# Two-head scores over 64 rows each, DMA transposes in the loop, and the PSUM banks dealt anew, in a hybrid decoder layer on eight cores

## Chip, cores and metric

The kernel runs on all 8 cores of one Trainium2 chip (two dies of four cores). The metric is the device time in microseconds of the slowest core. The cores don't talk to each other: each computes half of one of the four sequences (4096 of 8192 tokens) and recomputes what it needs of the 2048 tokens before its half.

## What is computed

One decoder layer over x of 4 x 8192 tokens by 1024 channels:

```python
h = rmsnorm(x, g_mix)
q, k, v, u, qm = split(h @ w_in)            # 512, 512, 512, 256, 256 columns
# A) 8 heads of 64: causal dilated windows (128,1), (512,4), (2048,16), each a softmax
#    with ALiBi bias; the three merged by their softmax denominators
# B) trailing means over 2/4/8/16 tokens minus the token, times w_pool, times pool_scale
# C) 4 heads of 64: cross-attention into 256 memory tokens (rmsnorm(mem) @ w_mem_kv)
x = x + concat(A, B, C) @ w_out
a = relu(rmsnorm(x, g_ffn) @ w_ff1)         # 4096 wide
x = x + (a * a) @ w_ff2
return rmsnorm(x, g_final)
```

## The kernel before

A core walks over 12 tiles of 512 tokens: tiles 0 to 3 are the halo (only K and V are made), tiles 4 to 11 its own. There is no scheduler: the order in which the program is written is the order on every engine. A small tracker (`Tracker`, L50) puts semaphore waits before each instruction for what it reads and overwrites; TensorE never waits for itself. Every engine takes its instructions strictly in that order, and so does SyncE's queue (SP), which issues most DMAs.

**Tile j** has these parts in time:

- *Stage B* (L539): 16 groups of 8 matmuls (K = 128, 512 columns) for the projections, four groups for each of four 1 MB weight pieces. VectorE writes Q as bf16, scaled. Q is written twice: `QA` has heads of even number in rows 0 to 63 and zeros below, `QB` heads of odd number in rows 64 to 127 and zeros above (L564, L569; `qmA` and `qmB` at L582 and L587 for the memory heads). K lies with two heads over one another in 128 rows (`KT`). Hooks in stage B (L964 to L968, at groups 1, 4, 6, 8 and, for the last norm, 2) turn the normalised rows of the tile before (`hb`) into `h2T`, the FFN's input: `stage_J_pe`, L797.
- *The mix* (`slot_mix`, L911): 64 groups of 8 matmuls of the FFN of tile j-1, and between them the attention of tile j, item by item. A batch is four score matmuls of 128 columns (or one of 512 for the memory heads) into one PSUM bank, `exp` on ScalarE (L680), a multiplication by a mask on VectorE (L689), and four value matmuls into a bank `ob` (L706). A tile has 8 heads x 7 batches and 4 memory heads x 2. An item issues the front of batch i (scores, exp, mask) and the back (value matmuls) of batch i - lag. In the mix too, at g = 7, 21, 35, 49, the normalised rows of tile j+1 are transposed into `hT` (`stage_A_pe`, L507).
- *Stage IJ* (L806): the output projection, 8 groups of 8 matmuls.

**Transposes** are done by `transpose_to` (L425): for a chunk of 128 tokens 8 TensorE transposes of 128x128 into the one bank `tp`, then one VectorE copy. There are three `hb` buffers (L209); `hT` and `h2T` are one buffer each, with one record of readers and writers for all four chunks.

**PSUM** has eight banks: mm0, mm1, sc0 to sc2, ob0, ob1 and tp. The FFN takes mm0 and mm1 in turn, the scores the three sc banks (five, with mm, in tile 4, which has no FFN beside it), the value sums ob[h % 2]. In stages B and IJ all of mm and sc serve as targets.

**Weights** come in 1 MB bf16 pieces through a ring of three buffers. SP issues each load when TensorE has read the buffer's last piece (`ring_issue`, L377). Before that, during tiles 0 to 5, GpSimd's queue converts the fp32 weights to bf16 in DRAM by DMA. From tile 7 on x is loaded by GpSimd's queue (L287).

In the last tile no stage B stands between stage IJ and the FFN: the four chunks are transposed at L1004 to L1007, and then the FFN runs alone.

Of the kernel before, what the change touches and what calls it, by code (L numbers as in the profile page):

```python
# [122 lines left out]
def build_nc(n_own=NOWN, debug=False):  # L123
# [27 lines left out]
    with ExitStack() as es:  # L151
# [84 lines left out]
        scb = [psum(f"sc{i}", [128, 4, 128], F32) for i in range(3)]  # L236
        b_sc = [Buf(f"sc{i}") for i in range(3)]
# [3 lines left out]
        b_ob = [Buf(f"ob{i}") for i in range(2)]  # L241
# [297 lines left out]
        def stage_B(j, ghooks=None):  # L539
# [5 lines left out]
            for ip, pi in enumerate(plist):  # L545
# [5 lines left out]
                for ol in range(4):  # L551
# [11 lines left out]
                    if pi == 0:  # L563
                        T.op("dve", lambda: nc.vector.tensor_scalar(  # L564
                            out=QA[:, ol, :].rearrange("p (r c) -> p r c", r=4),
                            in0=m_[:, :].rearrange("p (c r) -> p r c", r=4), scalar1=csm_t[:, 5:6], scalar2=None,
                            op0=ALU.mult),
                            reads=[bm_, b_g], writes=[b_Q])
                        T.op("dve", lambda: nc.vector.tensor_scalar(  # L569
                            out=QB[:, ol, :].rearrange("p (r c) -> p r c", r=4),  # L570
                            in0=m_[:, :].rearrange("p (c r) -> p r c", r=4), scalar1=csm_t[:, 6:7], scalar2=None,
                            op0=ALU.mult),
                            reads=[bm_, b_g], writes=[b_Q])
# [6 lines left out]
                    else:  # L580
# [3 lines left out]
                            in0=m_[:, :].rearrange("p (c r) -> p r c", r=4), scalar1=csm_t[:, 5:6], scalar2=None,  # L584
                            op0=ALU.mult),
                            reads=[bm_, b_g], writes=[b_qm])
                        T.op("dve", lambda: nc.vector.tensor_scalar(  # L587
                            out=qmB[:, mp, :].rearrange("p (r c) -> p r c", r=4),
                            in0=m_[:, :].rearrange("p (c r) -> p r c", r=4), scalar1=csm_t[:, 6:7], scalar2=None,
                            op0=ALU.mult),  # L590
                            reads=[bm_, b_g], writes=[b_qm])
# [504 lines left out]
```

How the kernel before makes its waits and increments, by code:

```python
    def wait(self, e, tok):  # L61
        if tok is None:
            return
        sem, val, prod = tok
        if prod == "pe" and e == "pe":
            return
        key = (e, id(sem))
        if self.waited.get(key, 0) >= val:
            return
        self.waited[key] = val
        self.eng[e].wait_ge(sem, val)
        self.nwaits += 1
# [16 lines left out]
    def op(self, e, fn, reads=(), writes=(), mark=True):  # L89
        self._pre(e, reads, writes)
        ins = fn()
        self.ninst[e] += 1
        if mark:
            self.cnt[e] += 1
            ins.then_inc(self.sem[e], 1)
            tok = (self.sem[e], self.cnt[e], e)
        else:
            tok = (self.sem[e], self.cnt[e] + 1, e)
        self._post(tok, reads, writes)
        return tok
# [1 line left out]
    def dma(self, e, dsem, out, in_, reads=(), writes=(), **kw):  # L102
# [2 lines left out]
        self.ninst[e] += 1  # L105
        dsem.val += 16
        ins.then_inc(dsem.sem, 16)
        tok = (dsem.sem, dsem.val, "dma")
# [14 lines left out]
def build_nc(n_own=NOWN, debug=False):  # L123
# [878 lines left out]
                    mem_phase()  # L1002
        wide["on"] = False
        stage_J_pe(0)
        stage_J_end(NT - 1, 3)
        for tc in range(1, 4):
            stage_J_pe(tc)
        for f in ffn_items(NT - 1, None):
            f()
        for tc in range(NX1):
            nc.sync.wait_ge(out_sem[tc].sem, out_sem[tc].val)
        build_nc.stats = dict(ninst=dict(T.ninst), nwaits=T.nwaits, sbuf_left=nc.sbuf_bytes_remaining)
    return nc
```

## Time and profile before

| | us |
|---|---|
| median of 3 runs | 1693.33 (1692.15 to 1700.11) |
| the profiled execution, its own time | 1693.58 |
| its span, slowest core (1) | 1692.5 |
| spans of the eight cores | 1679.9 to 1692.5 |
| TensorE busy | 1587.7 (94%) |
| VectorE busy | 993.8 (59%) |
| ScalarE busy | 755.7 (45%) |
| a tile in the steady part (632 to 818) | 186.0 |

The span runs from the first to the last instruction of the slowest core; 1.1 us of the execution's time lie around it. A matmul's length in the trace includes its way through the array, so two that follow each other overlap: what one costs in a dense stream is the distance from start to start. "PEld" are the weight loads, which run beside matmuls. "L680" is line 680 of the kernel. The parts stand in the trace as: halo and the stage B of tile 4 to 140 us, its attention and output projection to 220, tile 5 to 445, tile 6 to 632, then one each 186 us, the last one's attention ending before 1561, and the lone FFN to the end.

### The profile page before, as it was taken

Reading aid. Unit: us, or ns where it says so; the run is one execution under the profiler, and the core shown is the slowest. Engines: PE = TensorE matmul, PEld = TensorE weight load, DVE = VectorE, ACT = ScalarE, POOL = GpSimd, SP = SyncE. Lnnn points to the kernel's source line nnn. Section 1 sums busy time; section 2 is a strip of 40 time slices with the busy share of each in tenths; the row PEclk is TensorE's granted clock in tenths of the full one; section 3 lists DMA queues with packets and bytes.
Section 4 is the critical chain, followed back from the end, with each engine's and each line's share of the span. In section 5 each row is a group of like instructions: output and inputs, shape, how many; then the busy total and the mean of one; then the engine's idle time right before and its main releaser. Section 6 shows DMA issues by size and latency. Waiting matters only on the chain.

```text
span 1692.5 us, 30487 instructions; the slowest of 8 cores (1679.9 to 1692.5 us)
## 1 busy us (share of the span) xinstructions
PE 1587.7 (94%) x10320; PEld 853.1 (50%) x10320; DVE 993.8 (59%) x1613; ACT 755.7 (45%) x1481; POOL 59.5 (4%) x103
## 2 busy tenths in 40 slices
PE   4897677899999999999999999999999999999997
PEld 2455433455455545554455545554555545554443
DVE  4557444555766566655676575665675575556344
ACT  3426613355345552546245543555255533555112
POOL 2000000000000000000000000000000010000000
PEclk9999788899999999999999999999999999999999
DMA  9999999963644455433635354435534373245343
GB/s 222 244 181 187 174 163 204 170 181 137 211 132 152 152 204 173 161 139 137 214 122 192 140 211 157 150 113 193 200 130 159 124 246 122 104 147 190 117 154 124
DMA packets 68950, 280.68 MB, mean 166 GB/s; under 512 B 6080, under 2 KB 27840, under 8 KB 46144
## 3 DMA queue, kind: packets, MB, share of 16 engines
q1 hardware_dynamic: 37008, 215.19, 37.6%
q0 software_dynamic: 31792, 63.54, 19.4%
q8 instruction: 87, 1.43, 0.3%
q14 instruction: 63, 0.52, 0.1%
HBM read 278.09 MB, written 39.85 MB: 188 GB/s over the span
## 4 chain that ended last, share of the span: by engine, by line
PE 84%; DMA 8%; DVE 3%; ACT 3%; issue 2%; SPq 0%; ACTq 0%; DVEq 0%; POOL 0%; POOLq 0%
PE mm L450 32%; PE mm L881 25%; PE sc L450 8%; PE ob L706 6%; PE sc L678 6%; DMA ring<-wscratch 6%; PE sc L814 4%; PE tp L427 2%; PE mm L814 1%; DMA ring<-w_in 1%; ACT tmp L403 1%; DVE hb L417 1%; ACT P L680 1%; DMA x<-xh 1%; DVE x L886 0%
## 5 line engine op out<-in xcount | busy, mean ns | idle before, releaser
L450 PE MATMUL mm<-h2T,ring 128*128 128x512 bf16 x2080 | 492.5, 382 | 12.3 <-DMA ring<-wscratch 11.3
L881 PE MATMUL mm<-ring,aT 128*128 128x512 bf16 x2048 | 475.8, 380 | 14.1 <-DMA ring<-wscratch 9.0
L680 ACT ACTIVATE P<-sc 128x512 bf16<-128x512 f32 x487 | 283.3, 595 | 240.2 <-PE sc L678 225.9
L862 DVE TENSOR_TENSOR aT<-tmp 128x512 bf16<-128x512 f32 x256 | 176.9, 691 | 249.5 <-ACT tmp L861 248.5
L450 PEld LDWEIGHTS mm<-h2T,ring 128*128 128x128 bf16 x2080 | 197.1, 99 | 220.9 <-issue 22.0
L881 PEld LDWEIGHTS mm<-ring,aT 128*128 128x128 bf16 x2048 | 192.9, 98 | 224.4 <-issue 27.0
L861 ACT ACTIVATE tmp<-mm 128x512 f32<-128x512 f32 x256 | 153.0, 598 | 326.2 <-PE mm L450 302.2
L886 DVE TENSOR_TENSOR x<-x,mm 128x512 f32<-128x512 f32 x256 | 175.6, 686 | 164.2 <-PE mm L881 159.1
L689 DVE TENSOR_TENSOR P<-P,E 128x512 bf16<-128x512 bf16 x448 | 186.0, 421 | 64.3 <-ACT P L680 62.3
L706 PE MATMUL ob<-P,Vd 128*128 128x128 bf16 x1792 | 177.0, 222 | 14.6 <-DVE P L689 14.4
L403 ACT ACTIVATE tmp<-x 128x1024 bf16<-128x1024 f32 x80 | 84.6, 1058 | 114.8 <-DVE x L819 54.3
L706 PEld LDWEIGHTS ob<-P,Vd 128*128 128x128 bf16 x1792 | 122.0, 100 | 21.9 <-issue 18.5
L450 PE MATMUL sc<-hT,ring 128*128 128x512 bf16 x488 | 112.6, 383 | 9.9 <-DMA ring<-wscratch 9.9
L678 PEld LDWEIGHTS sc<-QB,KT 128*128 128x128 bf16 x856 | 69.2, 110 | 40.6 <-issue 1.4
L537 ACT CAST Vd<-sc 128x512 bf16<-128x512 f32 x26 | 15.2, 586 | 164.2 <-PE sc L450 144.1
L814 PE MATMUL sc<-ring,yT 128*128 128x512 bf16 x384 | 87.8, 386 | 0.0
L678 PEld LDWEIGHTS sc<-QA,KT 128*128 128x128 bf16 x848 | 67.8, 110 | 39.6 <-issue 3.0
L450 PE MATMUL mm<-hT,ring 128*128 128x512 bf16 x344 | 83.5, 389 | 3.7 <-DVE hT L430 2.0
L678 PE MATMUL sc<-QB,KT 128*128 128x128 bf16 x856 | 83.9, 221 | 0.0
L678 PE MATMUL sc<-QA,KT 128*128 128x128 bf16 x848 | 81.7, 221 | 1.9 <-DVE QB L569 1.9
L427 PE MATMUL tp<-ident,hb 128*128 128x128 bf16 x656 | 53.6, 229 | 29.6 <-DVE hb L417 25.3
L450 PEld LDWEIGHTS sc<-hT,ring 128*128 128x128 bf16 x488 | 47.7, 99 | 66.2 <-issue 11.8
(99 smaller groups left out, 1224.3 us busy)
## 6 DMA issues: line engine op xcount, KB each, us to landing
ring<-wscratch SPq DMA_DIRECT2D x173, 1024.0 KB, 6.4
wscratch<-w_ff POOLq DMA_DIRECT2D x16, 1024.0 KB, 139.2
out<-x POOLq DMA_DIRECT2D x32, 512.0 KB, 5.8
x<-xh SPq DMA_DIRECT2D x28, 512.0 KB, 16.2
xa<-xh POOLq DMA_DIRECT2D x20, 512.0 KB, 6.5
x<-xh POOLq DMA_DIRECT2D x20, 512.0 KB, 8.6
Vd<-Vd SPq DMA_DIRECT2D x33, 192.0 KB, 5.9
xa<-xh SPq DMA_DIRECT2D x12, 512.0 KB, 15.5
```

The costliest lines, as they stand in the source:

```text
L403: T.op("act", lambda: nc.scalar.activation(out=jk[:].bitcast(BF16), in_=src, func=AF.Square, accum_out=ss), reads=[b_src], writes=[bs, bjk])
L427: T.op("pe", lambda: nc.tensor.transpose(tp[:, k * 128:(k + 1) * 128], hb[:, k * 128:(k + 1) * 128], ident[:]), reads=[b_hb, b_id], writes ...
L450: T.op("pe", lambda: nc.tensor.matmul(out_ap, lhsT=l, rhs=r, start=(i == 0), stop=(i == n - 1)), reads=reads, writes=[b_out], mark=(i == n ...
L678: T.op("pe", lambda: nc.tensor.matmul(o2, lhsT=l, rhs=r, start=True, stop=True), reads=bt["qk_reads"], writes=[bs_], mark=(i == n - 1))
L680: T.op("act", lambda: nc.scalar.activation(out=P_[:], in_=s_, func=AF.Exp, bias=bt.get("bias", 0.0)), reads=[bs_], writes=[bP_])
L689: T.op("dve", lambda: nc.vector.tensor_tensor(out=Pv, in0=Pv, in1=m, op=ALU.mult), reads=[bP_, b_E], writes=[bP_])
L706: T.op("pe", lambda: nc.tensor.matmul(oo, lhsT=l, rhs=r_, start=(bt["first"] and i == 0), stop=(bt["last"] and i == n - 1), skip_group_che ...
L814: T.op("pe", lambda: nc.tensor.matmul(m_[:], lhsT=yT[:, k, tc * 128:(tc + 1) * 128], rhs=pk[:, k, :], start=(k == 0), stop=(k == 7)), read ...
L861: T.op("act", lambda: nc.scalar.activation(out=rt[:], in_=m_[:], func=AF.Relu), reads=[bm_], writes=[brt])
L862: T.op("dve", lambda: nc.vector.tensor_tensor(out=aT[:, fl, :], in0=rt[:], in1=rt[:], op=ALU.mult), reads=[brt], writes=[b_aT[fl]])
L881: T.op("pe", lambda: nc.tensor.matmul(m_[:], lhsT=aT[:, fl, tc * 128:(tc + 1) * 128], rhs=rhs, start=(fl == 0), stop=(fl == 7)), reads=[b_ ...
L886: T.op("dve", lambda: nc.vector.tensor_tensor(out=xs, in0=xs, in1=m_[:], op=ALU.add), reads=[bm_], writes=[bx])
```

## The change

Three things change.

1. **Scores over 64 rows.** `QB` and `qmB` go; `QA` and `qmA` hold both heads, scaled by a constant. A score matmul of head h takes only its own 64 rows of K and Q (rows 0 to 63 for even h, 64 to 127 for odd). The batches of two heads form pairs; the front of a pair issues matmul i of the one and then matmul i of the other, into two banks. An item is now half a pair: one carries the front of pair i and the back of the first batch of pair i-1, the next one the back of the second batch. A tile has 32 pairs and 66 items (before 66 items of one batch each).
2. **PSUM.** Two sc banks and three ob banks (obank = h % 3); tile 4 has four score banks (two sc, two mm). The third bank ob2 takes the place of sc2 among the targets of stages B and IJ.
3. **DMA transposes.** For the chunks of tile 7 and later (`stage_A_pe`) and of the FFN input of tile 6 and later (`stage_J_pe`), SP issues one `dma_start_transpose` of a [128, 1024] chunk into `hT` or `h2T` instead. It waits for `hb` to be written and for what last wrote or read the target.

```diff
-        QB = sb("QB", [128, 4, TOK], BF16)
-        qmB = sb("qmB", [128, 2, TOK], BF16)
...
-        scb = [psum(f"sc{i}", [128, 4, 128], F32) for i in range(3)]
+        scb = [psum(f"sc{i}", [128, 4, 128], F32) for i in range(2)]
...
-        ob = [psum(f"ob{i}", [128, 4, 128], F32) for i in range(2)]
+        ob = [psum(f"ob{i}", [128, 4, 128], F32) for i in range(3)]
...
+        tr_sem = [dsem(f"trsem{i}") for i in range(NHB)]
+
+        def dma_transpose_to(hb, b_hb, dst3, b_dst):
+            i = [k for k in range(NHB) if b_hbs[k] is b_hb][0]
+            T._pre("sp", [b_hb], [b_dst])
+            ins = nc.sync.dma_start_transpose(out=dst3, in_=hb[:])
+            T.ninst["sp"] += 1
+            tr_sem[i].val += 16
+            ins.then_inc(tr_sem[i].sem, 16)
+            T._post((tr_sem[i].sem, tr_sem[i].val, "dma"), [b_hb], [b_dst])
...
-        mm_all += [(t_.rearrange("p a b -> p (a b)"), b_) for t_, b_ in zip(scb[:3], b_sc[:3])]
+        mm_all += [(t_.rearrange("p a b -> p (a b)"), b_) for t_, b_ in zip(scb[:2], b_sc[:2])]
+        mm_all += [(ob[2][:].rearrange("p a b -> p (a b)"), b_ob[2])]
...
         def stage_A_pe(j, c):
             h_, bh_ = a_hb.pop((j, c))
             hd, b_hd = hbuf(j)
-            transpose_to(h_, bh_, hd[:, :, c * 128:(c + 1) * 128], b_hd)
+            tr = dma_transpose_to if j >= NHALO + 3 else transpose_to
+            tr(h_, bh_, hd[:, :, c * 128:(c + 1) * 128], b_hd)
...
                         T.op("dve", lambda: nc.vector.tensor_scalar(
                             out=QA[:, ol, :].rearrange("p (r c) -> p r c", r=4),
-                            in0=m_[:, :].rearrange("p (c r) -> p r c", r=4), scalar1=csm_t[:, 5:6], scalar2=None,
+                            in0=m_[:, :].rearrange("p (c r) -> p r c", r=4), scalar1=0.125, scalar2=None,
                             op0=ALU.mult),
-                            reads=[bm_, b_g], writes=[b_Q])
-                        T.op("dve", lambda: nc.vector.tensor_scalar(
-                            out=QB[:, ol, :].rearrange("p (r c) -> p r c", r=4),
...
+                            reads=[bm_], writes=[b_Q])
...
-        def attn_items(j, lag, nsc):
+        def attn_items(j, nsc):
...
-                Qz = (QA if hh == 0 else QB)[:, pr, :]
+                p0 = 64 * hh
+                Qz = QA[p0:p0 + 64, pr, :]
                 v0 = pr * 192 + 64 * hh
-                o_ = ob[h % 2]
+                o_ = ob[h % 3]
...
-                        kv = KT[:, pr, slot * TOK:(slot + 1) * TOK].rearrange("p (a s) -> p a s", s=4)[:, :, r]
+                        kv = KT[p0:p0 + 64, pr, slot * TOK:(slot + 1) * TOK].rearrange("p (a s) -> p a s", s=4)[:, :, r]
...
+            def emit_front(bts):
+                fr = []
+                for bt in bts:
+                    si = cnt["sc"] % nsc
+                    cnt["sc"] += 1
+                    pi = cnt["P"] % NPB
+                    cnt["P"] += 1
+                    bt["P"] = (Pbuf[pi], b_P[pi])
+                    fr.append((bt, scb[si], b_sc[si]))
+                n = len(bts[0]["qk"])
+                for i in range(n):
+                    for bt, s_, bs_ in fr:
+                        sec, l, r = bt["qk"][i]
...
+                        T.op("pe", lambda: nc.tensor.matmul(o2, lhsT=l, rhs=r, start=True, stop=True),
+                             reads=bt["qk_reads"], writes=[bs_], mark=(i == n - 1))
+                for bt, s_, bs_ in fr:
+                    P_, bP_ = bt["P"]
+                    T.op("act", lambda: nc.scalar.activation(out=P_[:], in_=s_, func=AF.Exp, bias=bt.get("bias", 0.0)),
+                         reads=[bs_], writes=[bP_])
...
+            pairs = []
+            for a in range(6):
+                half = 7 if a < 4 else 2
+                base = 14 * a if a < 4 else 56 + 4 * (a - 4)
+                for i in range(half):
+                    pairs.append((batches[base + i], batches[base + half + i]))
             items = []
-            n = len(batches)
-            for i in range(n + lag):
-                def item(i=i):
+            n = len(pairs)
+            for i in range(n + 1):
+                def item0(i=i):
                     if i < n:
-                        emit_front(batches[i])
+                        emit_front(pairs[i])
                     flush_post()
-                    if i >= lag:
-                        emit_back(batches[i - lag])
-                items.append(item)
+                    if i >= 1:
+                        emit_back(pairs[i - 1][0])
+
+                def item1(i=i):
+                    flush_post()
+                    if i >= 1:
+                        emit_back(pairs[i - 1][1])
+                items += [item0, item1]
             return items
...
-        def stage_J_pe(tc):
+        def stage_J_pe(j, tc):
             h_, bh_ = j_hb.pop(tc)
-            transpose_to(h_, bh_, h2T[:, :, tc * 128:(tc + 1) * 128], b_h2T)
+            tr = dma_transpose_to if j >= NHALO + 2 else transpose_to
+            tr(h_, bh_, h2T[:, :, tc * 128:(tc + 1) * 128], b_h2T)
...
-            lag = 3 if first else 2
-            at = attn_items(j, lag, 5 if first else 3)
+            at = attn_items(j, 4 if first else 2)
```

## Rows read from the trace of the kernel before

**Rows 1.** The page: busy us of the engines, clock and DMA in slices.
```profile
PE 1587.7 (94%) x10320; PEld 853.1 (50%) x10320; DVE 993.8 (59%) x1613; ACT 755.7 (45%) x1481; POOL 59.5 (4%) x103
...
PEclk9999788899999999999999999999999999999999
DMA  9999999963644455433635354435534373245343
```

**Rows 2.** Busy us by stretch: PE, PEld, DVE, ACT, POOL; then clock, DMA share, GB/s.
```profile
265.00:350.00 85.00, 68.12 (x475) 38.27 (x476) 41.80 (x75) 33.66 (x63) 0.00 (x0) 0.88 1.00 187
632.00:818.00 186.00, 185.25 (x1235) 100.31 (x1236) 117.35 (x193) 89.78 (x174) 6.35 (x12) 1.00 0.47 163
```

**Rows 3.** PE's waits from 204 to 450 us: total, times, longest
```profile
PE mm L450 <- DMA ring<-wscratch: 11.3, 2, 7.6
PE sc L450 <- DMA ring<-wscratch: 9.1, 1, 9.1
PE mm L881 <- DMA ring<-wscratch: 9.0, 3, 5.3
```

**Rows 4.** PE's waits from 450 to 1540 us
```profile
PE mm L881 <- DVE x L886: 3.7, 6, 0.6
```

**Rows 5.** Timeline of PE inside a mix: start us, us, instructions
```profile
700.56 1.89 PE L450 MATMUL mm<-h2T,ring 128*128 128x512 bf16 x8
702.28 0.39 PE L678 MATMUL sc<-QA,KT 128*128 128x128 bf16 x4
702.51 0.39 PE L706 MATMUL ob<-P,Vd 128*128 128x128 bf16 x4
702.73 1.89 PE L450 MATMUL mm<-h2T,ring 128*128 128x512 bf16 x8
```

**Rows 6.** Timeline of the weight loads there
```profile
702.46 0.26 PEld L706 LDWEIGHTS ob<-P,Vd 128*128 128x128 bf16 x4
```

**Rows 7.** Groups by line and shape: busy us, mean ns of one, idle before
```profile
L678 PE MATMUL sc<-QB,KT 128*128 128x128 bf16 x856 | 83.9, 221 | 0.0
...
L678 PE MATMUL sc<-QA,KT 128*128 128x128 bf16 x848 | 81.7, 221 | 1.9 <-DVE QB L569 1.9
...
L427 PE MATMUL tp<-ident,hb 128*128 128x128 bf16 x656 | 53.6, 229 | 29.6 <-DVE hb L417 25.3 <-DVE h2T L430 4.4
...
L569 DVE TENSOR_SCALAR QB<-mm,csm_t 128x512 bf16<-128x512 f32 x16 | 12.0, 751 | 1.7
```

**Rows 8.** Timeline of PE at a memory-token score and value matmul
```profile
598.32 0.38 PE L678 MATMUL sc<-qmA,kmT 128*128 128x512 bf16 x1
...
598.54 0.38 PE L706 MATMUL ob<-P,vmA 128*128 128x512 bf16 x1
```

**Rows 9.** Timeline of PE around one transposed chunk in stage B
```profile
632.06 1.89 PE L450 MATMUL mm<-hT,ring 128*128 128x512 bf16 x8 [0.77 <-DMA ring<-wscratch]
633.79 0.61 PE L427 MATMUL tp<-ident,hb 128*128 128x128 bf16 x8
634.23 1.89 PE L450 MATMUL mm<-hT,ring 128*128 128x512 bf16 x8
```

**Rows 10.** Timeline of PE, first feed-forward group of that tile
```profile
661.47 1.89 PE L450 MATMUL mm<-h2T,ring 128*128 128x512 bf16 x8
```

**Rows 11.** DMA issues from 632 to 818 us: KB each, median us to landing
```profile
x<-xh POOLq DMA_DIRECT2D x4, 512.0 KB, 9.2
...
Vd<-Vd SPq DMA_DIRECT2D x4, 192.0 KB, 5.6
```

**Rows 12.** Copies between tiles in SBUF over the whole span
```profile
DMA to landing us min/median/max: 4.4/5.9/21.3
```

**Rows 13.** Timeline of PE after a long wait for a ring piece
```profile
237.04 3.57 PE L450 MATMUL sc<-hT,ring 128*128 128x512 bf16 x8 [9.13 <-DMA ring<-wscratch]
```

**Rows 14.** Timeline of PE at the last tile's transposes
```profile
1560.87 0.61 PE L427 MATMUL tp<-ident,hb 128*128 128x128 bf16 x8
...
1569.91 15.90 PE L450 MATMUL mm<-h2T,ring 128*128 128x512 bf16 x64 [1.01 <-DVE h2T L430]
```

More of the change, by code:

```diff
@@ L583, in stage_B @@
                             out=qmA[:, mp, :].rearrange("p (r c) -> p r c", r=4),
-                            in0=m_[:, :].rearrange("p (c r) -> p r c", r=4), scalar1=csm_t[:, 5:6], scalar2=None,
+                            in0=m_[:, :].rearrange("p (c r) -> p r c", r=4), scalar1=0.125, scalar2=None,
                             op0=ALU.mult),
[L586 to L591, printed above, removed]
+                            reads=[bm_], writes=[b_qm])
                 if own and (j > NHALO or ip == 0):
@@ L630, in attn_items @@
                                         meng="dve",
-                                        pv=pv, pv_reads=[b_Vd4[slot]], obank=h % 2,
+                                        pv=pv, pv_reads=[b_Vd4[slot]], obank=h % 3,
                                         first=(dl == 0), last=False, post=None))
@@ L656, in attn_items @@
                 mp, hh = mh // 2, mh % 2
-                Qz = (qmA if hh == 0 else qmB)[:, mp, :]
+                p0 = 64 * hh
+                Qz = qmA[p0:p0 + 64, mp, :]
                 v0 = mp * 192 + 64 * hh
                 for kc in range(2):
-                    batches.append(dict(qk=[(None, kmT[:, mp, kc * 128:(kc + 1) * 128], Qz)],
+                    batches.append(dict(qk=[(None, kmT[p0:p0 + 64, mp, kc * 128:(kc + 1) * 128], Qz)],
                                         qk_reads=[b_km, b_qm], mask=None, meng=None,
@@ L662, in attn_items @@
                                         pv=[(None, vmA[:, kc, v0:v0 + 128], None)],
-                                        pv_reads=[b_vm], obank=mh % 2, first=(kc == 0), last=(kc == 1),
+                                        pv_reads=[b_vm], obank=(8 + mh) % 3, first=(kc == 0), last=(kc == 1),
                                         post=(6 + mh // 2, hh) if kc == 1 else None))
-            def emit_front(bt):
-                si = cnt["sc"] % nsc
-                cnt["sc"] += 1
-                pi = cnt["P"] % NPB
-                cnt["P"] += 1
-                s_, bs_ = scb[si], b_sc[si]
-                P_, bP_ = Pbuf[pi], b_P[pi]
-                n = len(bt["qk"])
-                for i, (sec, l, r) in enumerate(bt["qk"]):
-                    o2 = s_[:, sec, :] if sec is not None else s_.rearrange("p a b -> p (a b)")
-                    if len(r.shape) == 3:
-                        o2 = o2.rearrange("p (a b) -> p a b", a=r.shape[1])
-                    T.op("pe", lambda: nc.tensor.matmul(o2, lhsT=l, rhs=r, start=True, stop=True),
-                         reads=bt["qk_reads"], writes=[bs_], mark=(i == n - 1))
-                T.op("act", lambda: nc.scalar.activation(out=P_[:], in_=s_, func=AF.Exp, bias=bt.get("bias", 0.0)),
-                     reads=[bs_], writes=[bP_])
-                if bt["mask"] is not None:
-                    m = bt["mask"]
-                    Pv = P_[:].rearrange("p (a b) q -> p a b q", a=2) if len(m.shape) == 4 else P_[:]
-                    if bt["meng"] == "pool":
-                        T.op("pool", lambda: nc.gpsimd.tensor_tensor(out=Pv, in0=Pv, in1=m, op=ALU.mult),
-                             reads=[bP_, b_E], writes=[bP_])
-                    else:
@@ new lines, in emit_front @@
+            def emit_front(bts):
[11 more added lines that the diff above has]
+                        sec, l, r = bt["qk"][i]
+                        o2 = s_[:, sec, :] if sec is not None else s_.rearrange("p a b -> p (a b)")
+                        if len(r.shape) == 3:
+                            o2 = o2.rearrange("p (a b) -> p a b", a=r.shape[1])
+                        T.op("pe", lambda: nc.tensor.matmul(o2, lhsT=l, rhs=r, start=True, stop=True),
[4 more added lines that the diff above has]
+                         reads=[bs_], writes=[bP_])
+                    if bt["mask"] is not None:
+                        m = bt["mask"]
+                        Pv = P_[:].rearrange("p (a b) q -> p a b q", a=2) if len(m.shape) == 4 else P_[:]
```

24 lines of the change are left out of this document (10 added, 14 removed).

## The prediction, made before the changed kernel ran

> **What bounds the kernel now.** I read the page first: TensorE is busy 94% of the span, VectorE 59%, ScalarE 45%. Its slices show two regimes: eight slices of 42.3 us in which the DMA engines are full and the granted clock falls below 1.0 at times, and then, to the end, a TensorE at nine tenths and DMA at three to six [rows 1]. The busy times by stretch say the same: up to 350 us DMA has a share of 1.00 and TensorE gaps, a steady tile (632 to 818) has TensorE busy 185.3 of 186 us, DMA at 0.47, VectorE at 117 [rows 2]. Who is waited for: between 204 and 450 us TensorE waits 29.4 us for ring pieces (11.3 + 9.1 + 9.0) [rows 3]; between 450 and 1540 us its longest wait is 3.7 us in all [rows 4]. So from about 350 us on only fewer TensorE slots shorten the kernel. Before that a saved slot mostly lengthens a wait for weights.
>
> What a slot is, the timeline shows, not the mean durations. In the mix 8 matmuls of 512 columns take 702.28 - 700.56 = 1.72 us, four of 128 columns 0.22 us (702.28 to 702.51 to 702.73) [rows 5]: 56 ns a matmul, though the group's mean says 221 ns [rows 7]. Their weight loads keep that pace, four in 0.26 us [rows 6]. A steady tile adds up from this: stages B and IJ and the FFN 88 groups x 1.73 = 152 us, 448 attention matmuls x 0.056 = 25.1, 16 memory matmuls x 0.22 [rows 8] = 3.5, 8 chunks of transposes x 0.45 = 3.6, together 184 of 186.
>
> **The change, part by part.**
>
> *Scores.* There are 856 + 848 score matmuls into sc, and 88 more into mm in tile 4, 1792 in all [rows 7], or 224 a tile: 224 x 0.056 = 12.5 us, and 8 memory scores x 0.22 = 1.7 us. Number and columns stay the same, only the rows halve. If the two halves of the array work side by side, half of the 14.2 us goes, 7.1 a tile; if they don't, nothing. I take 6.5 tiles (half of tile 5 lies past 350 us; 6 to 11 whole): 0 to -46 us. I choose the full overlap, since the loads already overlap each other [rows 6] and the alternating heads have other rows and other banks.
>
> *Entering and leaving the 64-row form.* Every front now sits between 128-row matmuls: 2 switches x 32 pairs x 6.5 tiles = 416. No row has one. Lower end: nothing. Upper end: the array runs empty at each, which is the part of a matmul that lies beyond its slot, 0.38 - 0.22 = 0.16 us [rows 8]: +67 us. I take one slot of 128 columns, 0.056 us, as the time for one wave to leave: +23 us. It is nearest in size to what changes, a short matmul. What the Trainium skill says here (TensorEngine Tiling (Array Packing), Key Properties) speaks against the change: switching the tiling mode, other than switching tiles, drains TensorE. By that rule, with the 0.16 us that a row gives for a way through the array, this term is +67 instead of +23; no row here shows a switch.
>
> *TensorE transposes.* A chunk costs 634.23 - 633.79 = 0.45 us of TensorE [rows 9]. Gone are stage A for tiles 7 to 11 (20 chunks) and stage J for tiles 6 to 10 (20): 40 x 0.45 = -18 us; four more in the last tile are counted below. The 44 copies out of tp and the 48 writes of QB and qmB (0.75 us each [rows 7]) leave VectorE. That is priced at nothing: TensorE hardly waits for VectorE in that part [rows 4], and without them it is only idler.
>
> *The DMA transposes in their place.* 256 KB from SBUF to SBUF each. Nearest row: the copies Vd<-Vd, also within SBUF and also SP's, 192 KB, 5.6 us in the steady tile; the longest median there is 9.2 us [rows 11], the extremes over the span are 4.4 and 21.3 [rows 12]. I take L = 5.6 us. In the mix they have 30 us and more until stage B reads hT: nothing. In stage B the four are a chain, since each waits for the last writer of h2T, that is, for its predecessor to land. SP's order is: first transpose (start of the stage), the ring load that waits for group 3, second, third, the ring load that waits for group 7, fourth, ring load for group 11, Vd copies, ring load. The second is issued at 7.2 us at the earliest (four groups of 1.73, and a little), and the fourth lands at 7.2 + 3L = 24.0 us. The FFN, which reads h2T, begins 661.47 - 632.06 = 29.4 us into the stage now [rows 9, 10], 27.6 without the four transposes. So at 5.6 us they are hidden with 3.6 us to spare, the limit being L = 6.8. Queued behind the third is the ring load for group 7, which may start at 14 us and is held to 7.2 + L = 12.8: no loss. VectorE's last norm waits for the first transpose to free its hb, 5.6 us into the stage, about when it runs now.
>
> *The last tile* has no such cover. Today it takes 1569.91 - 1560.87 = 9.0 us from the first transpose to the first FFN matmul [rows 14]. With the chain it is 4 x 5.6 = 22.4 us: +13.4 (L = 4.4: +8.6; L = 9.2: +27.8). The clock after such a pause is no new cost: 8 matmuls took 3.57 us after a 9.13 us wait [rows 13], the lower of the two levels, 1.2 GHz, but the last FFN starts slow today as well, 64 matmuls in 15.9 us instead of 13.8 [rows 14].
>
> *Pipeline and banks.* A front now asks for both sc banks. They were emptied by two exps of 0.6 us, and the next front comes two FFN groups later, 3.4 us: cover enough, and the value matmuls of a pair come as late. With three ob banks a head's bank is used again after its division has had three items. Tile 4 has no FFN beside it and goes from a lag of three batches to one pair; what it gains or loses stands in front of the 29.4 us of ring waits [rows 3]. All priced at nothing.
>
> **Sum:** 1693.6 (this execution; the median of the three runs is 1693.3, so no correction) - 46 - 18 + 23 + 13 = 1666 us.
>
> **Rivals.**
>
> *R1, the switches eat it (slower).* Place: both ends of each front. At 0.16 us each: 1693.6 - 46 - 18 + 67 + 13 = 1710. It decides from (46 + 18 - 13) / 416 = 0.12 us a switch; below that the kernel gains. For: loads today run ahead of the matmuls without a gap [rows 6], which only holds while the form stays the same. Against: the only thing that speaks for a full drain is outside this trace. 17%.
>
> *R2, no overlap (the change doesn't do what it says).* The 64-row matmuls follow each other at 56 ns as before, switching is free: 1693.6 - 18 + 13 = 1689. For: in the rows a matmul's slot is its columns and nothing else (0.22 for 4 x 128 as for 1 x 512) [rows 5, 8]. Against: nothing ties the second head's stream to the first's. 15%.
>
> *R3, long transposes.* If L is 9.2 us, the fourth lands at 7.2 + 27.6 = 34.8, 7.2 us late, in 5 tiles: +36; the end costs 27.8 instead of 13.4. With the score terms as forecast: 1693.6 - 46 + 23 - 18 + 36 + 28 = 1717. It decides from L = 6.8 us (late h2T) and is worse than before from about 8.0 us. For: the chain of four and the margin of 3.6 us. Against: the copy next to it takes 5.6 and moves three quarters as much. 10%. The Trainium skill gives two answers (VectorE: DVE Perf Modes, The three transpose paths: 1309 ns for a 128x128 block; Advanced Engine Details and Errata, X-Bar Transpose: as fast as regular DMAs). By the first, eight blocks one after another are an estimated 10.5 us, and the sum would be about 1740; by the second the forecast stands. No row here shows either.
>
> **How the numbers follow.** Forecast 58%, R1 17%, R2 15%, R3 10%. The forecast's own range is 1638 (free switches, L = 4.4) to 1689 (0.11 us a switch). The whole range reaches over R2 to R1 and the price of R3 above: 1638 to 1715; what is left out is a switch over 0.16 us and anything below free switches. 0.5% (8.5 us, about what a measurement can tell) parts the signs at 1685 and 1702: the forecast all but 3 points and a few of R2 are faster, 0.60; most of R2, and R1 with a switch of about 0.12, same, 0.15; R1 and R3 slower, 0.25.
>
> **What the profile after would show.** Right: in the mix the 8 score matmuls of a pair start within about 0.25 us, and the next 128-row matmul less than 0.1 us late on either side; a steady tile of 186 - 7.1 + 3.6 - 3.6 = 179 us; 1.73 us between groups of stage B; transposes landing in 4.4 to 6.8 us; some 22 us between the last IJ matmul and the lone FFN. Wrong: score starts 56 ns apart (R2); holes of 0.1 us or more before and after each front (R1); TensorE waiting for a DMA into h2T after stage B, or for ring pieces held back on SP (R3). New waits for exp or the ob banks would contradict what I priced at nothing.

## The result, and the profile after

| | before | after |
|---|---|---|
| median of 20 runs each, us | 1691.61 | 1700.24 |
| ratio | | 1.0051 (95%: 1.0028 to 1.0075) |
| profiled execution, us | 1693.58 | 1702.65 |
| its span, slowest core | 1692.5 (core 1) | 1701.6 (core 2) |

The ratios here and below leave out executions in a slower state, in which the cores of one die show a lower granted clock. The change costs 0.5%, where 1.6% less was forecast. The page after, busy time and slices (as in [rows 1]; the second line is TensorE's):

```profile
PE 1578.3 (93%) x9968; PEld 768.4 (45%) x9968; DVE 937.6 (55%) x1521; ACT 747.3 (44%) x1481; POOL 59.5 (3%) x103
...
PE   4897788899999999999999999999999989995897
...
PEclk9997689899999999999999999999999999998999
DMA  9999999963547456535846374646753583336333
```

TensorE is still the bound; behind 350 us it is clearly idle in two places, the slice from 1361 us (0.8) and the one from 1531 us (0.5). Where the 9.1 us of span come from, by the first matmul of each part in the two traces (the last column takes the median of the eight cores before and after, since the slowest core is not the same one):

| stretch | before | after | difference | of the medians |
|---|---|---|---|---|
| start to stage B of tile 4 (halo) | 105.7 | 108.8 | +3.1 | +0.2 |
| to stage B of tile 7 | 526.4 | 521.7 | -4.7 | +0.9 |
| to stage B of tile 11 (four tiles) | 743.6 | 734.5 | -9.1 | -9.0 |
| to stage IJ of tile 11 | 171.4 | 177.1 | +5.7 | +6.9 |
| to the lone FFN | 22.9 | 35.5 | +12.6 | +11.5 |
| to the end | 122.6 | 124.1 | +1.5 | +0.9 |

**The mix.** TensorE's timeline of the changed kernel at the place of [rows 5]:

```profile
700.35 1.89 PE L460 MATMUL mm<-h2T,ring 128*128 128x512 bf16 x8
702.17 0.41 PE L685 MATMUL sc<-QA,KT 64*128 64x128 bf16 x8
702.52 0.40 PE L710 MATMUL ob<-P,Vd 128*128 128x128 bf16 x4
702.75 1.89 PE L460 MATMUL mm<-h2T,ring 128*128 128x512 bf16 x8
```

The FFN's last slot ends at 700.35 + 1.73 = 702.07, the value matmuls begin at 702.52: 0.45 us for a pair's eight scores, what they took before (8 x 0.056). Inside it the time is spent otherwise. The last FFN matmul and the first score, by a narrow stretch of the same view:

```profile
701.86 0.38 PE L460 MATMUL mm<-h2T,ring 128*128 128x512 bf16 x1
702.17 0.24 PE L685 MATMUL sc<-QA,KT 64*128 64x128 bf16 x1
```

and the weight loads, a front's eight in 0.26 us, then none until the value matmuls, in the 128-row form again:

```profile
702.16 0.26 PEld L685 LDWEIGHTS sc<-QA,KT 64*128 64x128 bf16 x8 [0.42 <-issue]
702.51 0.23 PEld L710 LDWEIGHTS ob<-P,Vd 128*128 128x128 bf16 x4
```

The single records start at 702.170 and .173, .254 and .257, .310 and .313, .365 and .369, then 702.517: the two heads run side by side, 3 to 4 ns apart, and from the second two matmuls on, each two start 56 ns after the two before. That is the saving, 4 x 0.056 = 0.22 us. Against it stand 702.170 - 702.074 = 0.096 on entering, 0.084 - 0.056 = 0.028 behind the first two, 702.517 - 702.421 = 0.096 on leaving, 0.010 behind the first value matmul: 0.23 us for one round of entering and leaving. In [rows 6] the loads ran ahead of the matmuls; across a change of form none does (the 0.42 us before the first). The page TensorEngine Tiling (Array Packing) of the Trainium skill, Key Properties, says that changing the tiling mode drains TensorE. The trace agrees in that no load of the new form runs ahead and each change costs about 0.115 us. A full drain it doesn't show: the first score starts at 702.170, before the end of the last FFN matmul's record (701.86 + 0.38 = 702.24, though such ends are modelled).

**The DMA transposes.** The transposes into h2T (who waited for them, and landing times), and the waits of TensorE from 450 us on:

```profile
  DVE hb L415: 39.4, 6
  PE mm L460: 21.5, 1
...
DMA to landing us min/median/max: 3.0/4.9/14.7
```

```profile
PE mm L460 <- DMA h2T<-hb: 21.5, 1, 21.5
PE sc L460 <- DVE QA L575: 5.3, 1, 5.3
...
PE ob L460 <- DMA ring<-wscratch: 1.8, 1, 1.8
```

In the loop h2T was never late for the FFN. What is late is hb, the source: with three buffers the fourth norm of a tile needs the first one's buffer, and waits for its transpose to land. The timeline at the start of stage B of tile 11 (SPq is SP's queue; its lines span from the first issue to the end of the last):

```profile
1363.53 2.05 SPq L104 DMA_DIRECT2D ring<-wscratch  x2
...
1365.68 5.49 SPq L436 DMA_TRANSPOSE h2T<-hb  x1
...
1380.51 1.28 DVE L415 SCALAR_TENSOR_TENSOR hb<-x,stat,gb_ffn 128x1024 bf16<-128x1024 f32 x1 [11.02 <-DMA h2T<-hb]
...
1382.54 1.86 PE L460 MATMUL sc<-hT,ring 128*128 128x512 bf16 x4 [5.28 <-DVE QA L575]
```

Two ring loads (2 MB) are issued, the transpose stands right behind them and lands 14.7 us later; VectorE waits 11.0 us, the PSUM banks fill, TensorE waits 5.3 us and comes back at the lower clock level (four matmuls in 1.86 us, where eight take 1.89).

Two ring loads stand in front of the first transpose in every stage B, and yet it doesn't always land so late. What differs is what GpSimd's queue moves meanwhile:

| first transpose into h2T, in | issued at | landed after, us | on GpSimd's queue until then |
|---|---|---|---|
| stage B of tile 7 | 631.2 | 7.2 | nothing |
| stage B of tile 8 | 814.1 | 11.5 | three stores of `out` |
| stage B of tile 9 | 999.6 | 7.5 | nothing |
| stage B of tile 10 | 1182.7 | 8.0 | nothing |
| stage B of tile 11 | 1365.7 | 14.7 | two stores of `out`, three loads of x |
| last tile's end | 1556.6 | 11.3 | three stores of `out` |

Over the eight cores it landed in 7.2 to 9.6 us in the 19 cases with nothing there, and in 13.9 to 17.8 us in tile 11, with four to six such transfers. No run changed this traffic, so it is an association. Tile 8 has the stall in a smaller form: its stage B takes 29.9 us instead of 27.6, mainly because the ring load issued just before the first transpose takes 10.1 us to land, instead of 5.6 in tile 7, and TensorE waits 1.8 us for it (on the eight cores that stage takes 29.5 to 31.9 us). The end of the last tile:

```profile
1554.14 1.89 PE L830 MATMUL ob<-ring,yT 128*128 128x512 bf16 x8
...
1556.59 18.87 SPq L436 DMA_TRANSPOSE h2T<-hb  x4
...
1568.02 1.28 DVE L415 SCALAR_TENSOR_TENSOR hb<-x,stat,gb_ffn 128x1024 bf16<-128x1024 f32 x1 [9.05 <-DMA h2T<-hb]
1577.53 2.72 PE L460 MATMUL mm<-h2T,ring 128*128 128x512 bf16 x6 [21.49 <-DMA h2T<-hb]
```

The first, again behind ring loads, takes 11.4 us (1556.6 to 1568.0), the other three 9.5 together (to 1577.5).

### The profile page after: what moved, and what is told of

It is laid out like the page before. It is cut to its first block, busy times and chain, and to the rows that moved or that the text cites. A ratio compares the mean times of both kernels' runs of the same rounds, so it can differ in the third digit from the quotient of the medians.

```text
span 1701.6 us, 29917 instructions; the slowest of 8 cores (1690.3 to 1701.6 us)
## 1 busy us (share of the span) xinstructions
PE 1578.3 (93%) x9968; PEld 768.4 (45%) x9968; DVE 937.6 (55%) x1521; ACT 747.3 (44%) x1481; POOL 59.5 (3%) x103
## 2 busy tenths in 40 slices
DMA packets 115413, 292.19 MB, mean 172 GB/s; under 512 B 52544, under 2 KB 74304, under 8 KB 92608
## 4 chain that ended last, share of the span: by engine, by line
PE 80%; DMA 10%; DVE 3%; ACT 3%; issue 3%; SPq 0%; ACTq 0%; DVEq 0%; POOL 0%; POOLq 0%
PE mm L460 29%; PE mm L897 25%; PE ob L710 8%; DMA ring<-wscratch 5%; PE sc L460 5%; PE sc L685 4%; PE sc L830 3%; PE ob L460 3%; DMA x<-xh 2%; DMA h2T<-hb 2%; PE mm L830 2%; PE ob L830 1%; DMA ring<-w_in 1%; ACT tmp L877 1%; DVE aT L878 1%
## 5 line engine op out<-in xcount | busy, mean ns | idle before, releaser
L689 ACT ACTIVATE P<-sc 128x512 bf16<-128x512 f32 x480 | 260.1, 596 | 238.5 <-PE sc L685 232.0
L878 DVE TENSOR_TENSOR aT<-tmp 128x512 bf16<-128x512 f32 x256 | 177.1, 692 | 268.8 <-ACT tmp L877 267.5
L401 ACT ACTIVATE tmp<-x 128x1024 bf16<-128x1024 f32 x80 | 84.5, 1056 | 119.2 <-DVE x L835 54.4
L685 PE MATMUL sc<-QA,KT 64*128 64x128 bf16 x1680 | 88.6, 226 | 1.0 <-DVE QA L575 1.0
L685 PEld LDWEIGHTS sc<-QA,KT 64*128 64x128 bf16 x1680 | 53.8, 110 | 78.4 <-issue 75.8
L460 PE MATMUL sc<-hT,ring 128*128 128x512 bf16 x352 | 82.1, 385 | 5.4 <-DVE QA L575 5.3
L725 DVE TENSOR_TENSOR yT<-ob,tmp 64x512 bf16<-64x512 f32 x96 | 65.9, 686 | 12.9 <-ACT tmp L721 10.7
L548 ACT CAST Vd<-sc 128x512 bf16<-128x512 f32 x15 | 8.8, 585 | 145.8 <-PE sc L460 126.9
L719 ACT ACTIVATE tmp<-ob 64x512 f32<-64x512 f32 x96 | 56.7, 591 | 18.5 <-PE ob L710 16.6
L721 ACT ACTIVATE tmp<-tmp 64x512 f32<-64x512 f32 x96 | 60.3, 628 | 9.4 <-ACT tmp L719 0.7
L415 DVE SCALAR_TENSOR_TENSOR hb<-x,stat,gb_ffn 128x1024 bf16<-128x1024 f32 x32 | 40.9, 1279 | 39.4 <-DMA h2T<-hb 39.4
L830 PE MATMUL sc<-ring,yT 128*128 128x512 bf16 x256 | 59.4, 385 | 0.3 <-DVE yT L725 0.3
## 6 DMA issues: line engine op xcount, KB each, us to landing
x<-xh POOLq DMA_DIRECT2D x20, 512.0 KB, 12.1
```

The source lines that it names most:

```text
L401: T.op("act", lambda: nc.scalar.activation(out=jk[:].bitcast(BF16), in_=src, func=AF.Square, accum_out=ss), reads=[b_src], writes=[bs, bjk])
L460: T.op("pe", lambda: nc.tensor.matmul(out_ap, lhsT=l, rhs=r, start=(i == 0), stop=(i == n - 1)), reads=reads, writes=[b_out], mark=(i == n ...
L685: T.op("pe", lambda: nc.tensor.matmul(o2, lhsT=l, rhs=r, start=True, stop=True), reads=bt["qk_reads"], writes=[bs_], mark=(i == n - 1))
L689: T.op("act", lambda: nc.scalar.activation(out=P_[:], in_=s_, func=AF.Exp, bias=bt.get("bias", 0.0)), reads=[bs_], writes=[bP_])
L725: "dve", lambda: nc.vector.tensor_tensor(out=yT[lo:lo + 64, ychunk, :], in0=of[lo:lo + 64, :], in1=rc[lo:lo + 64, :], op=ALU.mult),
L830: T.op("pe", lambda: nc.tensor.matmul(m_[:], lhsT=yT[:, k, tc * 128:(tc + 1) * 128], rhs=pk[:, k, :], start=(k == 0), stop=(k == 7)), read ...
```

## Experiments

All ratios are to the kernel before, with 95% intervals. "Early" means that the transposes into h2T are issued as soon as their rows are ready, "no chain" that they don't wait for each other. There are three hb buffers where nothing else is said. "The mix" below is the stretch from the first matmul of a stage B to the first of stage IJ, 172.1 us before (transposes included), 169.2 after.

| kernel | ratio |
|---|---|
| changed | 1.0051 (1.0028 to 1.0075) |
| a1, TensorE transposes | 1.0020 (1.0011 to 1.0029) |
| a2, old scores, DMA transposes | 1.0030 (1.0018 to 1.0042) |
| a3, last tile by TensorE | 0.9998 (0.9989 to 1.0008) |
| a4, four hb | 1.0029 (1.0005 to 1.0052) |
| b1, heads not alternating | 1.0077 (1.0064 to 1.0090) |
| b2, fronts (the score matmuls of a pair) split in two | 1.0347 (1.0333 to 1.0360) |
| b3, 128 rows | 1.0107 (1.0087 to 1.0127) |
| b4, early issue | 1.0126 (1.0113 to 1.0139) |
| d1, no chain, four hb | 0.9977 (0.9967 to 0.9987) |
| d2, old scores, no chain, early | 0.9940 (0.9926 to 0.9954) |
| d3, pairs, no chain, early, four hb | 0.9996 (0.9987 to 1.0006) |
| d4, two pairs a front, no chain, early, four hb | 1.0056 (1.0043 to 1.0069) |
| e1, pairs, no chain, early in the last tile alone, four hb | 0.9923 (0.9898 to 0.9949) |
| e2, old scores, the same, three hb | 0.9949 (0.9934 to 0.9964) |

### The two halves of the change (a1, a2)

```diff
-            tr = dma_transpose_to if j >= NHALO + 3 else transpose_to
+            tr = transpose_to
```

(and the same in `stage_J_pe`).

> The changed kernel with all transposes back on TensorE; scores, pairs and banks as changed. Theory 1 (the scores are a draw: two heads overlap and save 4 x 0.056 = 0.22 us a pair, entering and leaving the 64-row form costs 0.096 + 0.028 + 0.096 + 0.010 = 0.23 us): a ratio to the kernel before of 0.999 to 1.004, a steady tile of 186 to 187 us, no wait for h2T. Theory 2 (the new order of items, the shorter lag or the banks cost time of their own): 1.006 or more, with new waits of TensorE for exp, masks or value banks.

1.0020, a steady tile of 186.0 to 186.4 us against 185.9. The scores are a draw, slightly on the losing side: 32 x (0.454 - 0.448) = 0.2 us a tile. In the profiles more than that stands in tiles 4 and 5 (+1.6 and +1.5 us, medians of the eight cores); why is not shown. a2 puts only `dma_transpose_to` into the kernel before:

> The kernel before with only the DMA transposes. Theory 1 (they save 2.9 us in each of five steady tiles, lose 12.6 us in the last tile, and now and then stall VectorE when the first one lands late behind two ring loads): 15 less, 13 to 20 more, so a ratio to the kernel before of 0.998 to 1.005. Theory 2 (the scores cost time of their own): below 0.998. In either, a steady tile of about 182 us.

1.0030, with a steady tile of 182.3 us: the transposes take 3.6 us from it, as forecast, and the changed kernel's 183.0 is 0.7 above that. TensorE waits 9.1 us for QB and 20.3 at the end. The parts add up, within intervals of this size: 0.0020 + 0.0030 = 0.0050, measured 0.0051. Both lose a little.

### The end and the stall (a3, a4)

```diff
-            tr = dma_transpose_to if j >= NHALO + 2 else transpose_to
+            tr = dma_transpose_to if NHALO + 2 <= j < NT - 1 else transpose_to
```

(in `stage_J_pe`)

> The changed kernel with the last tile's four chunks transposed by TensorE, the others by DMA as changed. If the serial chain at the end is where the gain goes, about 12 us come back: a ratio to the kernel before of 0.996 to 0.999. Rival (the end would be as long anyway, by the norms that come one after another): 1.003 to 1.006, like the changed kernel.

0.9998: 0.0053 x 1692 = 9.0 us of the 12 come back. (In its profile the stall of tile 11 was 6.2 us.)

```diff
-NHB = 3
+NHB = 4
```

> The changed kernel with four hb buffers instead of three, so that VectorE's last norm of a tile doesn't wait for the first DMA transpose to land. If these stalls (39.4 us of VectorE, one of which held TensorE for 5.3 us in the changed kernel's profile) cost time, 2 to 7 us come back: a ratio to the kernel before of 0.999 to 1.004. In the last tile it changes nothing, since the four transposes still follow each other. Rival (the stalls are covered): as the changed kernel, 1.003 to 1.007.

1.0029, some 4 us less, though the intervals overlap. The trace is clear: no wait of VectorE for a transpose to land, and the mix of tile 11 takes 169.2 us instead of 177.1. The late ring piece in tile 8 stays (3.2 us), and so does the end:

```profile
PE mm L460 <- DMA h2T<-hb: 20.7, 1, 20.7
```

### What the 64-row form costs and gives (b1, b2, b3, d4)

b1 issues one head's four matmuls and then the other's:

```diff
-                for i in range(n):
-                    for bt, s_, bs_ in fr:
+                for bt, s_, bs_ in fr:
+                    for i in range(n):
```

> The changed kernel with the four score matmuls of the first head issued one after the other and then those of the second; same 64-row forms, same banks, same number of switches. If the alternation is what makes the halves overlap, the overlap is nearly all lost: 0.224 us a pair for 28 pairs and 0.216 for 4 memory pairs (which are single matmuls and alternate as before, so perhaps not lost), over 6.5 to 7 tiles about +40 us: 1.02 to 1.03. Rival (the halves overlap whatever the order, or don't overlap): 1.003 to 1.007, as the changed kernel.

The rival holds. TensorE's timeline of b1 is that of the changed kernel:

```profile
701.31 0.42 PE L685 MATMUL sc<-QA,KT 64*128 64x128 bf16 x8
701.66 0.40 PE L710 MATMUL ob<-P,Vd 128*128 128x128 bf16 x4
```

Eight in 0.35 us again, and the single starts still come in twos, 13 ns apart, so matmuls of the two row halves overlap even when four of one are issued before four of the other. (Of the eight, the two that raise a semaphore, the fourth and the last issued, are the last two to start.) The alternation is worth 10 ns a front: the mix is 169.4 to 169.5 us in an undisturbed tile, against 169.1 to 169.4. That is 0.001 of the 0.0026 by which b1 is slower; the intervals of the two overlap.

b2 puts the four value matmuls of an item (`mid`, the back of the first batch of pair i-1) between the halves of a front:

```diff
                 for i in range(n):
+                    if i == 2 and mid is not None:
+                        mid()
+                        mid = None
                     for bt, s_, bs_ in fr:
```

> The changed kernel with each front of the 28 attention pairs cut in two, with the four value matmuls of 128 rows between the halves, so that the 64-row form is entered and left twice instead of once. If a round of entering and leaving costs 0.23 us, 28 x 0.23 = 6.4 us are added to a steady tile, over 6.5 tiles 42 us: a ratio to the kernel before of 1.025 to 1.035. Rival (the 0.1 us holes beside a front belong to its semaphore waits, not to the change of form): less than 1.012.

1.0347: the mix 174.9 us, 5.7 more in a tile for 28 more rounds, 0.20 us each. Timeline of b2:

```profile
702.23 1.89 PE L905 MATMUL mm<-ring,aT 128*128 128x512 bf16 x8
704.05 0.28 PE L688 MATMUL sc<-QA,KT 64*128 64x128 bf16 x4
704.27 0.40 PE L715 MATMUL ob<-P,Vd 128*128 128x128 bf16 x4
704.60 0.28 PE L688 MATMUL sc<-QA,KT 64*128 64x128 bf16 x4
704.82 1.90 PE L905 MATMUL mm<-ring,aT 128*128 128x512 bf16 x8
```

Four scores, which side by side are worth 2 x 0.056 us, take 0.22 us, and from the first value matmul to the next score it is 0.33 us instead of 0.22. Tile 4, without FFN, grows too, by 15 us, which is the rest.

b3 has 128 rows again (`QB`, `qmB` and their writes restored, K unsliced):

```diff
-                Qz = QA[p0:p0 + 64, pr, :]
+                Qz = (QA if hh == 0 else QB)[:, pr, :]
```

> The changed kernel with scores over 128 rows again (QA and QB with zeros, written twice), everything else as changed: pairs, alternation, banks, DMA transposes. If the 64-row form is a draw, the time stays as with it: a ratio to the kernel before of 1.001 to 1.006, the 8 score matmuls of a front 56 ns apart and no hole of 0.1 us beside them. Rival (the new order costs time and the 64-row form gains it back): above 1.008. Other rival (the 64-row form costs on balance): below 0.999.

1.0107, which meets the number of the first rival. Its mix is 169.1 us in an undisturbed tile, as after; the scores of a front, alone and in sequence (three of nine lines):

```profile
702.37 0.22 PE L697 MATMUL sc<-QA,KT 128*128 128x128 bf16 x1
702.42 0.22 PE L697 MATMUL sc<-QB,KT 128*128 128x128 bf16 x1
...
702.81 0.61 PE L722 MATMUL ob<-P,Vd 128*128 128x128 bf16 x8
```

702.37 to 702.81, 0.45 us, without holes. Order, banks and semaphore waits are those of the changed kernel, so its holes belong to the change of form. What b3 loses against the changed kernel is in stage B, in TensorE's waits:

```profile
PE mm L462 <- DMA h2T<-hb: 22.3, 1, 22.3
PE sc L462 <- DVE QB L582: 14.7, 4, 7.7
```

With two Q writes a group VectorE comes out of the stall behind the late transpose later, four times instead of once. Against b3, then, the 64-row form gains through the 48 writes that VectorE no longer makes, which I had priced at nothing. That this takes the DMA transposes, which stall VectorE, is argued: 128 rows in pairs with TensorE's transposes were not run. Against a2 the changed kernel gains nothing. a2 has the same 48 writes, transposes and three hb as b3 and differs from it in the order of the items and the banks; it is 0.0077 below b3 and 0.0021 below the changed kernel. So the rival's reason, that the new order costs time, stands: 0.6 us of it shows in the undisturbed mix (168.5 us in a2), the rest in stalls that are longer in b3, by what is not shown.

d4 enters the form half as often: 16 scores a front, four sc banks (tp in one of them), two value banks, eight P buffers (they hold the exps), on the transposes of d3 below:

```diff
+            quads = [pairs[2 * i] + pairs[2 * i + 1] for i in range(len(pairs) // 2)]
...
+                        if b == 0 and i < n:
+                            emit_front(quads[i])
```

> The same transposes, and fronts of two pairs: 16 score matmuls over 64 rows into four sc banks (tp shares the fourth, ob has two), eight P buffers, so that the 64-row form is entered and left 16 times a tile instead of 32. If a round of entering and leaving costs 0.23 us whatever stands between, 16 x 0.23 = 3.7 us go from a steady tile: against one pair a front 22 to 26 us less, a ratio to the kernel before of 0.974 to 0.982, and in the mix 16 score matmuls in about 0.68 us. Rival (bursts of four exps and masks, or two value banks, make TensorE wait): the gain is half or less, with waits for masks or value banks in the mix.

1.0056, where 0.974 to 0.982 was expected. Timeline of d4, and TensorE's longest wait in it from 450 to 1540 us:

```profile
668.08 1.89 PE L465 MATMUL mm<-h2T,ring 128*128 128x512 bf16 x8
669.90 0.64 PE L690 MATMUL sc<-QA,KT 64*128 64x128 bf16 x16
670.47 0.82 PE L465 MATMUL mm<-h2T,ring 128*128 128x512 bf16 x3
```

```profile
PE ob L715 <- DVE yT L730: 24.2, 25, 1.7
```

The front takes 670.47 - 668.08 - 1.73 = 0.66 us for 16, where two fronts of a pair take 0.91: the price of the form is per entry, as said. But the mix stays at 170 to 171 us: with two value banks TensorE waits 24.2 us for divisions in six tiles, 4.0 a tile, more than the 16 x 0.23 = 3.7 that was to be gained. Tile 4 lost 9 us against d3. With three value banks there is no room for four sc banks beside mm; that version was not tried.

### Where the transposes stand (b4, d1, d2, d3, e1, e2)

b4 issues them when their rows are ready:

```diff
                             stage_J_end(j, tc - 1)
+                            if j >= NHALO + 2 and tc < 3:
+                                stage_J_pe(j, tc - 1)
-            ring_issue()
-            ring_issue()
+            if j < NT - 1:
+                ring_issue()
+                ring_issue()
+            if j >= NHALO + 2:
+                stage_J_pe(j, 2)
```

> The changed kernel with the FFN-input transposes issued as soon as their rows are normalised: the first two inside stage IJ, ahead of its two ring loads, the third right after those, the fourth at group 4 of stage B; in the last tile all four ahead of the ring loads. If the first transpose is late because it lands behind 2 MB of ring loads, and the end is the serial chain, then the stall of VectorE goes (3 us or so) and the end shrinks from 21.5 us of waiting to about 8: a ratio to the kernel before of 0.992 to 0.997. Rival (a transpose takes its 5 us and more wherever it stands): 1.000 or more.

1.0126, where 0.992 to 0.997 was expected. The stall is gone and the end shorter, but TensorE waits for the ring in every stage B (its waits, then SP's timeline at one):

```profile
PE ob L460 <- DMA ring<-wscratch: 19.7, 5, 7.4
PE mm L460 <- DMA h2T<-hb: 12.3, 1, 12.3
```

```profile
813.32 10.59 SPq L436 DMA_TRANSPOSE h2T<-hb  x2
824.06 0.94 SPq L104 DMA_DIRECT2D ring<-wscratch  x2
```

SP holds the second transpose until the first has landed, and the two ring loads, issued at 811.99 in the changed kernel, go at 824. I had looked at the place in the DMA queue and not at SP behind it. So d1 takes the chain away (the four write different columns; readers wait for all four), with four hb:

```diff
-            T._pre("sp", [b_hb], [b_dst])
+            T._pre("sp", [b_hb], [])
+            for t in b_dst.r:
+                T.wait("sp", t)
+            ws = [] if b_dst.r else b_dst.ws + [b_dst.w]
...
+            b_dst.ws = ws
```

> The changed kernel with four hb buffers, and a DMA transpose that no longer waits for its predecessor into the same h2T or hT (the four write different columns; readers wait for all four). Places of issue as changed. If the chain of landings is what fills the last tile, its four transposes follow each other at the 1.25 us that SP needs for one instead of 3.75 us, behind the ring loads: the wait before the lone FFN falls from 21 to 8 to 14 us, and the kernel by 7 to 13 us against the one with four hb buffers alone (1.0029): 0.995 to 0.999. Rival (the transposes are slow because the ring loads are ahead of them, and waiting together doesn't help): 1.002 to 1.004.

0.9977, 8.8 us less than a4; the wait at the end is 15.1 us instead of 20.7 (8 to 14 was expected). No stage B stalls by more than 1.6 us on any core, and the mix of tile 11 is 169.2. This is the first gain over the kernel before. d2 and d3 have the early issue of b4 without the chain, d2 on the kernel before with three hb, d3 on the changed one with four:

> Scores, banks and lag of the kernel before; DMA transposes without the chain, issued as soon as the rows are normalised (first two inside stage IJ ahead of the ring loads, third behind them, fourth at group 4 of stage B; in the last tile all ahead of the ring loads). If SP's waits for landings were what held back the ring loads when the transposes stood early (ring waits of 1.7 to 7.4 us in each stage B), these are gone: 5 tiles x 3 us less, last tile as before or 2 us less: a ratio to the kernel before of 0.988 to 0.993. Rival (the transposes take bandwidth from the ring whatever SP does): 0.998 or more.

> The same transposes with the changed kernel's scores (two heads over 64 rows, one pair a front) and four hb buffers. If the 64-row scores are a draw, this is as fast as with the old scores, up to 0.003 slower as it was with TensorE transposes: 0.988 to 0.996. Rival (they gain once VectorE is relieved in stage B): faster than with the old scores by over 0.003.

0.9940 and 0.9996, each just above what was expected. The wait at the end falls to 7.5 us in both. But ring waits remain (d2, then d3):

```profile
PE sc L467 <- DMA ring<-wscratch: 9.7, 3, 7.9
```

```profile
PE ob L466 <- DMA ring<-wscratch: 9.0, 2, 6.1
```

That left open whether the early issue in the loop costs them. e1 is d3 with it in the last tile alone (`if j == NT - 1 and tc < 3`), e2 the same with the old scores and three hb:

> The changed kernel with four hb buffers and no chain, and the transposes moved ahead of the ring loads in the last tile alone; in the loop they are issued at the hooks of stage B, as changed. If moving them ahead inside stage IJ costs the loop ring waits (9.0 us in the profile with the pairs, and 1.8 for the clock), while in the last tile it gains 7.5 us of waiting (15.1 to 7.5), this beats both kernels it is made of (0.9977 and 0.9996): 0.991 to 0.995, with less than 2 us of ring waits after 450 us. Rival (the ring waits come with the DMA transposes wherever they are issued): 0.996 or more.

> The same places of issue and no chain with the scores of the kernel before, and three hb buffers, for which alone there is room beside QB. VectorE's last norm then waits again for the first transpose, which lands behind two ring loads, with two Q writes a group behind it. If that stall is what the score form decides (9.1 us of TensorE waiting for QB with the DMA transposes alone, none with four buffers), this is slower than with the pairs and four buffers, by 2 to 10 us: 0.993 to 0.999. Rival (the pairs cost 0.002 to 0.005 here as well): faster than the other by 0.002 or more.

e1 0.9923, e2 0.9949; the intervals overlap. TensorE's waits in e1, then e2:

```profile
PE mm L466 <- DMA h2T<-hb: 7.5, 1, 7.5
...
PE ob L466 <- DMA ring<-wscratch: 1.3, 1, 1.3
```

```profile
PE sc L467 <- DVE QB L587: 11.9, 3, 7.9
```

e1 is below both kernels, by 0.8% and 1.3%. With the pairs the early issue in the loop costs time (d3 against e1), and belongs where nothing queues behind it. With the old scores it costs none (d2 0.9940, e2 0.9949): there it pays for its ring waits by ending the wait for QB, 11.9 us in e2 and none in d2. Whether e1 leads e2 by its scores or by its fourth hb is open, since the old scores with four hb and no chain were not run.

d3 is 0.006 above d2, when a1 gives the pairs only 0.002. Of the 7.2 us between the medians of the eight cores 4.8 lie in tile 8: its stage B takes 29.4 to 32.4 us in d3, with a ring piece late on every core, and 27.6 to 28.6 in d2. Why only there and only with the pairs is not settled.

## Why the prediction was wrong

- **The regime** was read right. From 204 to 450 us the ring waits are of the same kind and size (10.8 + 7.6 + 7.9 = 26.3 us against 29.4 [rows 3]), and from there on TensorE's slots set the time, but for the stalls below.
- **The overlap of the two heads**, -46 us: right, the starts are 3 to 4 ns apart. Of my reasons, the alternation hardly counts (b1).
- **The switches**: this step failed. "I take one slot of 128 columns, 0.056 us" measured 0.115 us (0.23 a round in the trace, 0.20 by b2). 416 x 0.115 = +48 us instead of +23. R1 was priced with 0.16 and was to decide from 0.12; the truth lies just under that point, so the scores come out at -46 + 48, nothing. No row had the term, and "the time for one wave to leave" was too little: no weight load runs ahead across a change, and the first matmul of the new form comes 0.096 us late, with 0.01 to 0.03 more behind it. The 0.16 us [rows 8] of a full drain would have been nearly as far off on the other side. R1 had the place and the sign right.
- **TensorE's transposes**: right, a steady tile lost 3.6 us by them alone (a2) and 2.9 in the changed kernel. "The copies are priced at nothing", and the writes of QB too: wrong once VectorE stalls (b3: TensorE waits 14.7 us for it against 5.3).
- **Their landing**: L = 5.6 us as one number was the second failed step. The range is 3.0 to 14.7 into h2T (5.9 to 14.5 into hT), by what else is moving. The fourth came in time, since the later ones of the chain are short. But "VectorE's last norm waits for the first transpose ..., about when it runs now" took the 5.6 for the one transpose that stands behind two ring loads, and that one took 7.2 at the least. Tile 11 took 5.7 us more to its stage IJ, where 1.8 less was to come from the transposes and 3.5 less from the scores.
- **The last tile**: +13.4 forecast, +12.6 measured, which is luck: not four equal landings of 5.6, but 11.4 and then 9.5 for three.
- **Pipeline and banks** at nothing: right in the loop as far as waits show (no new one for exp, masks or value banks above 1 us in all from 450 us on), but b3 against a2 leaves a cost of the new order that no term had. Tile 4 takes 1.6 us more (113.8 us against 112.2, medians of the eight cores), at a granted clock of 0.66 against 0.83 from 150 to 200 us.

With the measured switch the sum is 1693.6 - 46 - 18 + 48 + 13 = 1691, against 1702.7 measured. Of the 12 us between, about 10 are the stalls of tile 11 (+5.7 instead of -1.8) and of tile 8 (2.4). The rest is small: the 0.7 us by which each steady tile falls short, the start, 3.1 us more on another core, and what tiles 4 to 6 give back. The time lies in the whole range, where R1 is, on the wrong side of no change: R1's cost at a smaller price, plus a part of R3's cause, long landings, in another place.

## What to carry to other kernels

Halving the rows of small matmuls to run two at once pays only if the run in that form is long: here 8 matmuls of 128 columns save 0.22 us and pay 0.23 us to enter and leave, 16 save 0.45 and pay about the same once (d4's front; the kernel around it lost that again). A DMA that replaces engine work brings its landing into whatever reuses its source, and that landing depends on what its own queue issued just before and, it seems, on what other queues move; count buffers for it, and don't chain transfers that write different columns. Before moving a transfer forward, see what stands behind it on the issuing queue.

## What was unexpected of the hardware

- Two streams of matmuls on the two row halves overlap although one head's four are issued wholly after the other's (b1: starts 13 ns apart, eight in 0.35 us).
- A DMA transpose of [128, 1024] bf16 landed in 3.0 us at best, and behind two 1 MB loads in 7.2 to 14.7. It takes 1.2 us of SP at best, up to 5.5 behind them (7.6 in a4). The page VectorE: DVE Perf Modes of the Trainium skill (The three transpose paths) gives 1309 ns for a 128x128 block; eight one after another would be an estimated 10.5 us, which the 3.0 us contradict.
- The DMA packets of the core rose from 68950 to 115413, 1056 more for each of the 44 transposes, and the x loads on GpSimd's queue went from a median of 8.6 us to landing to 12.1.
